# Key and value tiles of a 512-token block: split before eviction, rate operations in short pieces, zeros and a few operations moved into the load phase

## The chip, the cores and the metric

One core of a Trainium2 chip. The metric is the device time of one execution, in microseconds, as the median of three runs.

## The reference

Two stacks of layers over 512 tokens of width 1024, in fp32. What matters here is the start: an attention layer with a compressed, a selected and a windowed branch, and behind it a state-space layer whose rates come from its parameters alone.

```
h = x
y = nsa_mixer(rmsnorm(h, l0_norm), l0_w_in, cmp_k_*, cmp_v_*, l0_w_out)
#   q, kc, vc, ks, vs, kw, vw, gates, z = split(hn @ w_in)
#   k_cmp = silu(blocks(kc) @ w1) @ w2, v_cmp alike: windows of 32 tokens, stride 16
h = h + y
y = s5_mixer(rmsnorm(h, l1_norm), ...)
#   dt = exp(log_dt); ab = exp(lambda * dt), complex: exp, sin, cos of [64, 64] parameters
#   coef = (ab - 1) / lambda; then a scan with powers of ab
h = rmsnorm(h + y, final_norm)
#   then two more layers (attention, gated linear attention) with gated feed-forwards
```

## The kernel before, in words

**Weights.** All weights are a stream of 288 tiles of 128 x 1024, in the order of the stages. SP loads tile t into raw[t mod 4] as soon as POOL has finished with what lay there. Every product is three fp32r matmuls of a high and a low half: DVE's `split_tile` copies raw into whi[t mod 2] (L171), POOL subtracts to get wlo[t mod 2] (L163, waits for w_hi), PE runs 24 matmuls of 512 columns per tile (three per chunk of 128, eight chunks) into one of two accumulators and counts `tile_done`. Since whi and wlo hold two tiles, DVE splits tile u + 2 once PE is through tile u, and PE needs POOL's low half of it one tile later.

**The first stage, nsa_kv,** has eight such tiles (keys and values of three branches; L1154 to L1156). The activations' high halves come from ACT (L1328), the low halves from DVE (L389). The gates are a small fp32 product in front of tile 0 and in its middle (L1140), whose weights `wgate` DVE first multiplies by the norm's gains (L1490). The norm's factor `rstd` needs all squares (ACT L224, DVE L237, PE L244 and L246), so tiles are multiplied by it afterwards: DVE's eviction (L1513) takes acc times rstd, to a bank for u < 4, to nk for the others, and frees the accumulator. For u < 4, ACT copies the high half, kvc_h (`high(u)`, L1347), and DVE subtracts the low half, kvc_l (L1518). After two tiles, ACT issues eight copies between SBUF tiles (`windows(0)`, then `windows(1)`, L1354) that lay out the windows x2 for the compression; they need zeros at the rims (n_zero). nmix is the gates times rstd (L1504).

**The second stage, cmp,** has eight tiles again, two per output, with matmuls of 160 columns (L1184 to L1186); it needs all sixteen copies. Beside it DVE and ACT redo the activations with rstd in them (L1532, L1537, L1360). Then comes nsa_rest, in wide matmuls again (L180 to L182).

**Beside these stages** DVE computes the rates of the state-space layer: some hundred operations on 128 x 32 elements, each of which waits for the one before it (`after_last`; L2157, L2161, L2165). `s5_early(dve, u)` hangs a piece of them behind each tile: u = 0 to 7 are the key and value tiles, 8 to 11 the first four of nsa_rest. Pieces before the change: u = 0 fraction (9 operations), 1 step (7), 2 magnitude (14), 3 angles reduced (13), 4 angles doubled (13 with its polynomial), 5 coefficients (18), 6 powers 0 to 2 (14), 8, 9 and 10 two powers each (12). Tile 4 has four more small ones for the position tables (L1524, L1526). The exponent's power of two is ACT's (L2142).

**What sets the order:** each engine runs its own list as written, and waits only on semaphores. A wait holds everything behind it on its engine; a DMA issue on ACT's queue holds what ACT does later. The loads before the start are issued by SP (weights tile 0, the two halves of x, weights tiles 1 to 3) and ACT (gains, tables, wgate, par, d, then nsa_tables, w2, pe).

Of the kernel before, what the change touches and what calls it, by code (L numbers as in the profile page):

```python
# [47 lines left out]
def build(nc, A, out, names=tuple(s[0] for s in STAGES)):  # L48
# [5 lines left out]
    with ExitStack() as ctx:  # L54
# [1077 lines left out]
        def nsa_loads(act):  # L1132
            for to, what in ((ntab, "nsa_tables"), (w2, "w2"), (pe_in, "pe")):
                act.dma_start(to[:], A[what]).then_inc(n_loaded, 16)

        def pe_nsa(pe):
# [4 lines left out]

            pe.wait_ge(n_wgate, 17)
# [23 lines left out]
            pe.wait_ge(n_loaded, 48)  # L1166
# [156 lines left out]
        def act_first_norm(act):  # L1323

            act.wait_ge(loaded, 32)

            def high(m):
                nc.scalar.activation(xh[:, m, :], h[:, m, :], ACT.Copy,  # L1328
                                     scale=gains[:, N_NSA, m:m + 1]).then_inc(norm_hi, 1)

            act.wait_ge(x_landed[0], 16)
            for m in range(4):
                high(m)
            for m in range(3):
                act_square(act, 0, m)
            act.wait_ge(x_landed[1], 16)
            for m in range(4, KC):
                high(m)
            for m in range(3, KC):
                act_square(act, 0, m)  # L1340
            act_rstd(act, 0)
            act_s5_pow2(act)

        def act_nsa(act):
# [24 lines left out]
            for u in range(3):  # L1369
                high(u)  # L1370
# [3 lines left out]
            act.wait_ge(n_zero, 8)  # L1374
            windows(0)
# [104 lines left out]
        def dve_nsa_begin(dve):  # L1480

            for kv in range(2):
                for part in range(2):
                    nc.vector.memset(x2[kv][part][:, 0:4, S - 1:S + 16].bitcast(F32), 0.0).then_inc(n_zero, 1)
                    nc.vector.memset(x2[kv][part][:, 4, :].bitcast(F32), 0.0).then_inc(n_zero, 1)
            nc.vector.memset(kcb[:], 0.0).then_inc(n_zero, 1)
            nc.vector.memset(vcb[:], 0.0).then_inc(n_zero, 1)
# [12 lines left out]
            for m in range(3, KC - 1):  # L1500
                dve_square_sum(dve, 0, m)
            s5_exponent(dve)
            dve.wait_ge(rstd_ready, 1)
            nc.vector.tensor_tensor(nmix[0:48, :], bank[2][0:48, :], rstd[0:48, :], ALU.mult).then_inc(n_gmm, 1)  # L1504

        def dve_nsa(dve):
            T = T0["nsa_kv"]
            for u in range(8):
                dve.wait_ge(tile_done, T + u + 1)
                if 2 <= u < 4:  # L1510
# [4 lines left out]
                split_tile(dve, (u + 2) % 4, (T + u + 2) // 4)  # L1515
# [4 lines left out]
                if u == 4:  # L1520
                    dve.wait_ge(n_loaded, 48)
# [148 lines left out]
        def pool_nsa(pool):  # L1670
# [8 lines left out]
            def slope(i):  # L1679
                if i == 0:  # L1680
                    pool.wait_ge(n_loaded, 48)
# [454 lines left out]
        def s5_early_loads(act):  # L2136
            for to, what in ((par, "s5_par"), (sd, "s5_d")):
                act.dma_start(to[:], A[what]).then_inc(s_loaded, 16)
# [41 lines left out]
        def s5_exponent(dve):  # L2180

            dve.wait_ge(s_loaded, 32)
# [20 lines left out]

        def s5_magnitude(dve):

            polynomial(dve, ee, xx, [1.0 / FACT[k] for k in range(7, 0, -1)])
# [4 lines left out]
        def s5_angles_reduced(dve):  # L2211
# [52 lines left out]
        def s5_coefficients(dve):  # L2264
# [8 lines left out]
            nc.vector.reciprocal(den, den).then_inc(s_par, 1)  # L2273
            for to, a, b, op in ((cre, nr, abim, ALU.add), (cim, abim, nr, ALU.subtract)):
# [520 lines left out]
        def _(pe):  # L2795
            pe.wait_ge(loaded, 32)
# [203 lines left out]
```

## Time and profile before

| | |
|---|---|
| median of 3 runs | 2107.71 us (2105.72 to 2107.86) |
| profiled execution | 2108.85 us, span 2107.1 us |
| mean granted TensorE clock | 0.972 |
| PE, busy share of the span | 95% |
| DVE, ACT, POOL | 55%, 29%, 38% |
| DMA | 167.64 MB, mean 80 GB/s |

The span is the time from the first to the last instruction of the profiled execution; the execution's own time has 1.75 us more around it. PE's busy share counts matmuls that wait in the pipeline too, so the stretches and the idle times in front of single instructions say more.

### The profile page before, as it was taken

What the parts mean: (1) busy time and instruction counts of PE and PEld (TensorE: products, weight loads), DVE (VectorE), ACT (ScalarE), POOL (GpSimd) and SP (SyncE); (2) the same over time, 40 slices, a digit from 0 to 9 for tenths busy, and PEclk for the clock granted to TensorE, in tenths of its full rate; (3) what the DMA queues carried; (4) which work ended last, traced back from release to release, by engine and by line L of the source; (5) the groups of instructions that cost most, each with busy time, mean ns of one, the idle gap of its engine ahead of it and who ended that gap; (6) DMA issues with size and microseconds to landing.
All of it is one profiled execution on the core that took longest, in us unless ns stands there. A gap on an engine that the chain in (4) does not pass through costs nothing.

```text
span 2107.1 us, 26825 instructions
## 1 busy us (share of the span) xinstructions
PE 1991.7 (95%) x9916; PEld 1562.5 (74%) x9916; DVE 1148.8 (55%) x2072; ACT 607.4 (29%) x1164; POOL 810.9 (38%) x420
## 2 busy tenths in 40 slices
PE   7999999787998996999999999999899999999999
PEld 4877777566777874666668888888578778888887
DVE  6748998576996434555465444522443355445411
ACT  3125566222553113454432111100332222111100
POOL 2441221244774443222224444444233334444444
PEclk9789999999999998999999999999999999999999
DMA  4520010111201222111112222233222222222231
GB/s 163 157 91 31 31 41 31 61 69 54 79 31 51 92 98 77 59 61 60 60 51 92 100 98 91 100 105 105 72 70 70 79 71 92 100 92 97 100 128 72
DMA packets 55300, 167.64 MB, mean 80 GB/s; under 512 B 8080, under 2 KB 16144, under 8 KB 54816
## 3 DMA queue, kind: packets, MB, share of 16 engines
q1 hardware_dynamic: 47904, 155.22, 21.3%
q10 hardware_dynamic: 7296, 11.08, 1.8%
q8 instruction: 65, 1.06, 0.2%
q14 instruction: 35, 0.29, 0.0%
HBM read 157.88 MB, written 2.10 MB: 76 GB/s over the span
## 4 chain that ended last, share of the span: by engine, by line
issue 40%; PE 32%; POOL 15%; DVE 10%; SPq 2%; ACT 0%; POOLq 0%; DMA 0%; DVEq 0%; ACTq 0%
POOL wlo L163 14%; PE bank L180 7%; PE bank L182 7%; PE bank L181 6%; SPq L145 2%; DVE prob L1628 2%; DVE ssb L1615 1%; PE bank L2576 1%; PE bank L2578 1%; PE bank L2577 1%; DVE sb__134 L2391 1%; DVE sb__134 L2386 1%; PE bank L1260 1%; PE bank L1285 1%; DVE sp__133 L2389 1%
## 5 line engine op out<-in xcount | busy, mean ns | idle before, releaser
L163 POOL TENSOR_TENSOR wlo<-raw,whi 128x1024 fp32r<-128x1024 f32 x252 | 606.5, 2407 | 990.4 <-DVE whi L171 990.4
L171 DVE CAST whi<-raw 128x1024 fp32r<-128x1024 f32 x288 | 203.4, 706 | 430.0 <-PE bank L182 235.3
L180 PE MATMUL bank<-xh,whi 128*128 128x512 f32 x704 | 277.0, 393 | 9.3 <-POOL wlo L163 9.3
L181 PE MATMUL bank<-xl,whi 128*128 128x512 f32 x704 | 275.9, 392 | 0.0
L182 PE MATMUL bank<-xh,wlo 128*128 128x512 f32 x704 | 275.6, 391 | 0.0
L595 PE MATMUL bank<-xh,whi 128*128 128x512 f32 x424 | 177.3, 418 | 1.5 <-POOL wlo L163 1.5
L597 PE MATMUL bank<-xh,wlo 128*128 128x512 f32 x424 | 165.9, 391 | 0.0
L596 PE MATMUL bank<-xl,whi 128*128 128x512 f32 x424 | 165.3, 390 | 0.0
L180 PEld LDWEIGHTS bank<-xh,whi 128*128 128x128 f32 x704 | 133.5, 190 | 38.3 <-POOL wlo L163 10.6
L181 PEld LDWEIGHTS bank<-xl,whi 128*128 128x128 f32 x704 | 133.6, 190 | 27.8
L182 PEld LDWEIGHTS bank<-xh,wlo 128*128 128x128 f32 x704 | 133.4, 190 | 28.0
L180 PE MATMUL bank<-ghi,whi 128*128 128x512 f32 x352 | 136.9, 389 | 0.0
L181 PE MATMUL bank<-glo,whi 128*128 128x512 f32 x352 | 136.9, 389 | 0.0
L182 PE MATMUL bank<-ghi,wlo 128*128 128x512 f32 x352 | 136.9, 389 | 0.0
L1676 POOL TENSOR_TENSOR wlo<-raw,whi 128x1024 fp32r<-128x1024 f32 x20 | 47.2, 2359 | 154.8 <-DVE whi L171 154.8
L595 PEld LDWEIGHTS bank<-xh,whi 128*128 128x128 f32 x424 | 79.7, 188 | 27.9 <-issue 13.4
L597 PEld LDWEIGHTS bank<-xh,wlo 128*128 128x128 f32 x424 | 79.6, 188 | 17.8
L596 PEld LDWEIGHTS bank<-xl,whi 128*128 128x128 f32 x424 | 79.9, 188 | 16.3 <-issue 2.2
L1628 DVE TENSOR_SCALAR prob<-prob,gsig,stat 128x128 f32<-128x128 f32 (+3 forms) x128 | 87.2, 723 | 2.3
L477 DVE TENSOR_TENSOR upad<-bank,rstd 128x512 f32<-128x512 f32 x44 | 30.5, 692 | 102.4 <-PE bank L182 87.4
L224 ACT ACTIVATE bank<-h 128x512 f32<-128x512 f32 x42 | 25.2, 602 | 209.7 <-DVE h L401 200.9
L490 DVE TENSOR_TENSOR bank<-bank,rstd 128x512 f32<-128x512 f32 x44 | 30.8, 700 | 99.5 <-PE bank L182 94.2
(384 smaller groups left out, 4030.9 us busy)
## 6 DMA issues: line engine op xcount, KB each, us to landing
raw<-in_weights_dram SPq DMA_DIRECT2D x288, 512.0 KB, 3.2
h<-in_x_dram SPq DMA_DIRECT2D x2, 1024.0 KB, 7.5
sz<-su SPq DMA_DIRECT2D x128, 16.0 KB, 1.8
out_dram<-h ACTq DMA_DIRECT2D x4, 512.0 KB, 2.6
etab<-in_even_tables_dram ACTq DMA_DIRECT2D x1, 1730.0 KB, 6.4
x_kh<-kvc_h ACTq DMA_DIRECT2D x2, 256.0 KB, 3.6
x_kl<-kvc_l ACTq DMA_DIRECT2D x2, 256.0 KB, 7.1
x_vh<-kvc_h ACTq DMA_DIRECT2D x2, 256.0 KB, 7.1
```

The source lines that it names most:

```text
L145: sp.dma_start(sz[32 * r:32 * r + 32, j, q * P:(q + 1) * P], su[32 * q:32 * q + 32, j, r * P:(r + 1) * P]).then_inc(s_ub[j % 4], 16)
L163: nc.gpsimd.tensor_tensor(wlo[:, s % 2, :], raw[:, s, :], whi[:, s % 2, :].bitcast(F32), ALU.subtract).then_inc(w_lo, 1)
L171: nc.vector.tensor_copy(whi[:, t_of_4 % 2, :], raw[:, t_of_4, :]).then_inc(w_hi, 1)
L180: nc.tensor.matmul(to, w_h, pe_h, start=first and k == 0, stop=False)
L181: nc.tensor.matmul(to, w_h, pe_l, start=False, stop=False)
L182: last_mm = nc.tensor.matmul(to, w_l, pe_h, start=False, stop=last and k == chunks - 1)
L490: nc.vector.tensor_tensor(gv, acc[1][:], rstd[:], ALU.mult).then_inc(acc_free[1], 1)
L595: nc.tensor.matmul(to[:], w_h, xh[:, k, :], start=k == 0, stop=False)
L596: nc.tensor.matmul(to[:], w_h, xl[:, k, :], start=False, stop=False)
L597: mm = nc.tensor.matmul(to[:], w_l, xh[:, k, :], start=False, stop=k == KC - 1)
L1628: mul = nc.vector.tensor_scalar(prob[:, br, hd, 0:w], prob[:, br, hd, 0:w], gsig[:, qb, g:g + 1], stat[:, 8 + 2 * br + hd:9 + 2 * br + hd] ...
L1676: nc.gpsimd.tensor_tensor(wlo[:, r % 2, :], raw[:, r % 4, :], whi[:, r % 2, :].bitcast(F32), ALU.subtract).then_inc(w_lo, 1)
```

## The change

1. In `dve_nsa` the split of tile u + 2 stands before the eviction of tile u, and nmix behind the first eviction.
2. The rate operations are cut anew. Exponent and fraction (2 and 9 operations) come before DVE's first wait for the loads, step (7) at the end of `dve_nsa_begin`. Then u = 0 exponential (7), 1 magnitude (7), 2 angles reduced (8), 3 sine and cosine (9), 4 angles doubled (9), 5 coefficients (7), 6 input coefficients (11), 7 nothing, 8 powers 0 to 2 (14), 9, 10 and 11 two powers each (12).
3. The ten memsets for n_zero move from DVE to POOL, ahead of its stream.
4. ACT's loads: par, gains, wgate, tables, ..., d last; ACT's power of two comes before its first wait for the loads.
5. PE runs four fp32 matmuls of 512 columns on a zeroed tile before the gates; its wait for the loads at the top is gone.
6. On ACT, `windows(0)` stands behind `high(1)` instead of behind the gates' sigmoid, so ahead of `high(2)`.

```diff
         def pe_nsa(pe):
...
+            pe.wait_ge(acc_free[0], 1)
+            pe.wait_ge(acc_free[1], 1)
+            for _ in range(4):
+                nc.tensor.matmul(acc[1][:], xf[:, 0, 0:P], xf[:, 0, :], start=True, stop=True)
             pe.wait_ge(n_wgate, 17)
...
         def act_first_norm(act):
 
+            act_s5_pow2(act)
             act.wait_ge(loaded, 32)
...
             act_rstd(act, 0)
-            act_s5_pow2(act)
...
-            for u in range(3):
-                high(u)
+            high(0)
+            high(1)
+            act.wait_ge(n_zero, 8)
+            windows(0)
+            high(2)
             nc.scalar.activation(bank[6], rstd[:], ACT.Copy).then_inc(n_gs, 1)
             act.wait_ge(n_gmm, 2)
             nc.scalar.activation(gsig[:].rearrange("p b g -> p (b g)"), bank[3][:, 0:4 * 48], ACT.Sigmoid).then_inc(n_gs, 1)
-            act.wait_ge(n_zero, 8)
-            windows(0)
             high(3)
             windows(1)
...
-        def dve_nsa_begin(dve):
+        def pool_zeros(pool):
...
+        def dve_nsa_begin(dve):
+
+            s5_exponent(dve)
+            s5_fraction(dve)
             dve.wait_ge(loaded, 32)
             dve.wait_ge(n_wgate, 16)
...
-            s5_exponent(dve)
-            dve.wait_ge(rstd_ready, 1)
-            nc.vector.tensor_tensor(nmix[0:48, :], bank[2][0:48, :], rstd[0:48, :], ALU.mult).then_inc(n_gmm, 1)
+            s5_step(dve)
 
         def dve_nsa(dve):
             T = T0["nsa_kv"]
             for u in range(8):
                 dve.wait_ge(tile_done, T + u + 1)
+                split_tile(dve, (u + 2) % 4, (T + u + 2) // 4)
+                if u == 0:
+                    dve.wait_ge(rstd_ready, 1)
                 if 2 <= u < 4:
                     dve.wait_ge(n_kvh, u - 1)
                     dve.wait_ge(n_kvl, u - 1)
                 nc.vector.tensor_tensor(bank[4 + u % 2] if u < 4 else nk[:, u - 4, :], acc[u % 2][:], rstd[:],
                                         ALU.mult).then_inc(acc_free[u % 2], 1)
-                split_tile(dve, (u + 2) % 4, (T + u + 2) // 4)
+                if u == 0:
+                    nc.vector.tensor_tensor(nmix[0:48, :], bank[2][0:48, :], rstd[0:48, :], ALU.mult).then_inc(n_gmm, 1)
...
         @block.gpsimd
         def _(pool):
             if "s5_in" in names:
+                pool_zeros(pool)
                 pool_stream(pool, 0, T0["nsa_rest"])
...
         @block.scalar
         def _(act):
+            s5_early_loads(act)
             act.dma_start(gains[:], A["gains"]).then_inc(loaded, 16)
+            act.dma_start(wgate[:], A["wgate"]).then_inc(n_wgate, 16)
             act.dma_start(tables[:], A["tables"]).then_inc(loaded, 16)
-            act.dma_start(wgate[:], A["wgate"]).then_inc(n_wgate, 16)
-            s5_early_loads(act)
...
         @block.tensor
         def _(pe):
-            pe.wait_ge(loaded, 32)
...
+            nc.vector.memset(xf[:, 0, :], 0.0)
```

What it moves on DVE, from the end of the first norm (spt, par: rate operations; whi<-raw: the split; bank<-bank,rstd: the eviction). Before:

```order
L2161 TENSOR_SCALAR spt<-spt 128x32
L1504 TENSOR_TENSOR nmix<-bank,rstd 48x512
L1513 TENSOR_TENSOR bank<-bank,rstd 128x512
L171 CAST whi<-raw 128x1024
L1518 TENSOR_TENSOR kvc_l<-bank,kvc_h 128x512
L2165 SCALAR_TENSOR_TENSOR spt<-spt,par 128x32
L2165 SCALAR_TENSOR_TENSOR spt<-spt 128x32
L2161 TENSOR_SCALAR spt<-spt 128x32
L2165 SCALAR_TENSOR_TENSOR spt<-spt 128x32 x6
L1513 TENSOR_TENSOR bank<-bank,rstd 128x512
```

And with the change:

```order
L2168 TENSOR_TENSOR spt<-par,spt 128x32
L2172 TENSOR_SCALAR spt<-spt 128x32
L171 CAST whi<-raw 128x1024
L1524 TENSOR_TENSOR bank<-bank,rstd 128x512
L1527 TENSOR_TENSOR nmix<-bank,rstd 48x512
L1530 TENSOR_TENSOR kvc_l<-bank,kvc_h 128x512
L2172 TENSOR_SCALAR spt<-spt 128x32
L2176 SCALAR_TENSOR_TENSOR spt<-spt 128x32 x6
L171 CAST whi<-raw 128x1024
L1524 TENSOR_TENSOR bank<-bank,rstd 128x512
```

The split is ahead of the eviction in every tile, and nine operations after kvc_l are seven.

On ACT behind the first norm (kvc_h<-bank: `high`; DMA x_kh, x_kl: `windows(0)`; x_vh, x_vl: `windows(1)`). Before:

```order
L256 ACTIVATE rstd<-lnv 128x512
L2142 ACTIVATE spt<-spt 128x32
L1347 ACTIVATE kvc_h<-bank 128x512 x3
L1371 ACTIVATE bank<-rstd 128x512
L1373 ACT_TABLE_LOAD
L1373 ACTIVATE gsig<-bank 128x192
L1354 DMA x_kh<-kvc_h 64x2x512 x2
L1354 DMA x_kh<-kvc_h 64x2x511 x2
L1354 DMA x_kl<-kvc_l 64x2x512 x2
L1354 DMA x_kl<-kvc_l 64x2x511 x2
L1347 ACTIVATE kvc_h<-bank 128x512
```

And with the change:

```order
L256 ACTIVATE rstd<-lnv 128x512
L1351 ACTIVATE kvc_h<-bank 128x512 x2
L1358 DMA x_kh<-kvc_h 64x2x512 x2
L1358 DMA x_kh<-kvc_h 64x2x511 x2
L1358 DMA x_kl<-kvc_l 64x2x512 x2
L1358 DMA x_kl<-kvc_l 64x2x511 x2
L1351 ACTIVATE kvc_h<-bank 128x512
L1378 ACTIVATE bank<-rstd 128x512
L1380 ACT_TABLE_LOAD
L1380 ACTIVATE gsig<-bank 128x192
L1351 ACTIVATE kvc_h<-bank 128x512
```

Eight copies stand between the second and the third kvc_h.

## Rows read from the trace of the kernel before

**Rows 1.** The page's row of the granted clock, 40 equal slices, tenths.
```profile
PEclk9789999999999998999999999999999999999999
```

**Rows 2.** Stretches: length, busy us (count) of PE, PEld, DVE, ACT, POOL, clock, DMA, GB/s.
```profile
35.05:38.05 3.00, 0.00 (x1) 0.00 (x0) 2.93 (x3) 0.57 (x1) 2.34 (x1) 1.00 0.00 0
38.05:41.60 3.55, 3.54 (x9) 2.77 (x10) 3.21 (x11) 0.60 (x1) 0.47 (x1) 0.53 0.46 152
...
67.85:69.03 1.18, 0.17 (x1) 0.00 (x0) 1.18 (x1) 0.00 (x0) 1.13 (x1) 1.00 1.07 239
...
74.60:76.66 2.06, 0.18 (x1) 0.00 (x0) 2.03 (x2) 0.00 (x0) 1.84 (x1) 1.00 0.00 0
76.66:79.20 2.54, 2.51 (x18) 2.54 (x19) 2.16 (x12) 0.00 (x0) 0.00 (x0) 1.00 0.56 200
79.20:82.99 3.79, 1.56 (x9) 1.34 (x8) 3.75 (x7) 1.19 (x2) 2.35 (x1) 0.50 0.02 9
82.99:119.10 36.11, 36.11 (x169) 36.11 (x170) 13.06 (x20) 6.48 (x13) 16.60 (x7) 0.50 0.31 108
119.10:123.50 4.40, 4.40 (x12) 3.43 (x12) 0.69 (x1) 0.54 (x2) 2.36 (x1) 0.50 0.19 74
```

**Rows 3.** Timeline of DVE at tile 0: start, length, instruction, idle before it.
```profile
33.70 0.68 DVE L1504 TENSOR_TENSOR nmix<-bank,rstd 48x512 f32<-48x512 f32 x1 [8.68 <-ACT rstd L256]
...
35.66 0.69 DVE L1518 TENSOR_TENSOR kvc_l<-bank,kvc_h 128x512 fp32r<-128x512 f32 x1
36.26 1.79 DVE L2165 SCALAR_TENSOR_TENSOR spt<-spt,par 128x32 f32<-128x32 f32 x1
...
38.52 1.32 DVE L2165 SCALAR_TENSOR_TENSOR spt<-spt 128x32 f32<-128x32 f32 x6
```

**Rows 4.** The same view at tile 6's eviction, DVE and POOL.
```profile
72.72 0.68 DVE L1513 TENSOR_TENSOR nk<-bank,rstd 128x512 f32<-128x512 f32 x1
...
73.32 0.69 DVE L171 CAST whi<-raw 128x1024 fp32r<-128x1024 f32 x1
...
74.09 2.35 POOL L163 TENSOR_TENSOR wlo<-raw,whi 128x1024 fp32r<-128x1024 f32 x1 [5.11 <-DVE whi L171]
```

**Rows 5.** The same view of the start: two issues on ACT's queue, DVE's first wait.
```profile
1.67 0.45 ACTq L2752 DMA_DIRECT2D wgate<-in_wgate_dram  x1
...
2.16 0.59 ACTq L2138 DMA_DIRECT2D par<-in_s_par_dram  x1
...
11.19 0.56 DVE L1490 TENSOR_TENSOR wgate<-wgate,gains 128x384 f32<-128x384 f32 x1 [7.21 <-DMA wgate<-in_wgate_dram]
```

**Rows 6.** DMA issues up to 20 us: KB each, us from issue to landing.
```profile
wgate<-in_wgate_dram ACTq DMA_DIRECT2D x1, 192.0 KB, 9.4
...
par<-in_s_par_dram ACTq DMA_DIRECT2D x1, 48.0 KB, 10.4
```

**Rows 7.** Timeline of PE: the gates' passes, before tile 0 and in it.
```profile
11.85 6.54 PE L1140 MATMUL bank<-h,wgate 128*48 128x512 f32 x8 [11.85 <-DVE wgate L1490]
21.27 3.63 PE L1140 MATMUL bank<-h,wgate 128*48 128x512 f32 x8
```

**Rows 8.** Timeline of ACT and its queue: the first copy of windows(0), then high(3).
```profile
46.22 0.72 ACTq L1354 DMA_DIRECT2D x_kh<-kvc_h  x1
...
53.83 0.60 ACT L1347 ACTIVATE kvc_h<-bank 128x512 fp32r<-128x512 f32 x1 [4.95 <-issue]
```

**Rows 9.** Instructions on kvc_l: count, ns of one min/median/max, first and last start.
```profile
L1354 ACTq DMA_DIRECT2D x_kl<-kvc_l x4: 628/913/1794, 49.4 to 53.2; - x4
L1354 ACTq DMA_DIRECT2D x_vl<-kvc_l x4: 636/710/942, 58.1 to 60.6; - x4
...
DMA to landing us min/median/max: 6.7/8.3/12.0
```

**Rows 10.** Timeline of DVE: its split behind the fourth tile of nsa_rest.
```profile
151.53 0.69 DVE L171 CAST whi<-raw 128x1024 fp32r<-128x1024 f32 x1 [6.12 <-PE bank L597]
```

More of the change, by code:

```diff
@@ L1132, in nsa_loads @@
         def nsa_loads(act):
-            for to, what in ((ntab, "nsa_tables"), (w2, "w2"), (pe_in, "pe")):
+            for to, what in ((ntab, "nsa_tables"), (w2, "w2"), (pe_in, "pe"), (sd, "s5_d")):
                 act.dma_start(to[:], A[what]).then_inc(n_loaded, 16)
@@ L1164, in pe_nsa @@
                     mm.then_inc(n_gmm, 1)
-            pe.wait_ge(n_loaded, 48)
+            pe.wait_ge(n_loaded, 64)
             pe.wait_ge(n_x2, 16 * 16)
@@ L1478, in act_macro @@
                 act_exps(act, M + 1, 1)
-        def dve_nsa_begin(dve):
+        def pool_zeros(pool):
             for kv in range(2):
                 for part in range(2):
[L1484 to L1487, printed above, removed]
+                    nc.gpsimd.memset(x2[kv][part][:, 0:4, S - 1:S + 16].bitcast(F32), 0.0).then_inc(n_zero, 1)
+                    nc.gpsimd.memset(x2[kv][part][:, 4, :].bitcast(F32), 0.0).then_inc(n_zero, 1)
+            nc.gpsimd.memset(kcb[:], 0.0).then_inc(n_zero, 1)
+            nc.gpsimd.memset(vcb[:], 0.0).then_inc(n_zero, 1)
+        def dve_nsa_begin(dve):
+            s5_exponent(dve)
+            s5_fraction(dve)
             dve.wait_ge(loaded, 32)
@@ L1520, in dve_nsa @@
                 if u == 4:
-                    dve.wait_ge(n_loaded, 48)
+                    dve.wait_ge(n_loaded, 64)
                     for kv in range(2):
@@ L1680, in slope @@
                 if i == 0:
-                    pool.wait_ge(n_loaded, 48)
+                    pool.wait_ge(n_loaded, 64)
                 if i >= 2:
@@ L2136, in s5_early_loads @@
         def s5_early_loads(act):
-            for to, what in ((par, "s5_par"), (sd, "s5_d")):
-                act.dma_start(to[:], A[what]).then_inc(s_loaded, 16)
+            act.dma_start(par[:], A["s5_par"]).then_inc(s_loaded, 16)
         def act_s5_pow2(act):
@@ L2180, in s5_exponent @@
         def s5_exponent(dve):
-            dve.wait_ge(s_loaded, 32)
+            dve.wait_ge(s_loaded, 16)
             ts(dve, kk, lg_dt, 1.4426950408889634, MAGIC, ALU.mult, ALU.add)
@@ L2202, in s5_step, with s5_exponential @@
             ts(dve, xx, xx, -80.0, 1.0 / 64, ALU.max, ALU.mult)
+        def s5_exponential(dve):
+            polynomial(dve, ee, xx, [1.0 / FACT[k] for k in range(7, 0, -1)])
         def s5_magnitude(dve):
-            polynomial(dve, ee, xx, [1.0 / FACT[k] for k in range(7, 0, -1)])
             for _ in range(6):
@@ L2273, in s5_coefficients, with s5_input_coefficients @@
             nc.vector.reciprocal(den, den).then_inc(s_par, 1)
+        def s5_input_coefficients(dve):
             for to, a, b, op in ((cre, nr, abim, ALU.add), (cim, abim, nr, ALU.subtract)):
@@ L2331, in s5_early @@
             if u == 0:
-                s5_fraction(dve)
+                s5_exponential(dve)
             if u == 1:
-                s5_step(dve)
+                s5_magnitude(dve)
             if u == 2:
-                s5_magnitude(dve)
+                s5_angles_reduced(dve)
             if u == 3:
-                s5_angles_reduced(dve)
+                s5_sine_cosine(dve)
             if u == 4:
@@ L2343, in s5_early @@
             if u == 6:
+                s5_input_coefficients(dve)
+            if u == 8:
                 s5_powers(dve, 0, 2)
-            if u == 8:
+            if u == 9:
                 s5_powers(dve, 3, 4)
-            if u == 9:
+            if u == 10:
                 s5_powers(dve, 5, 6)
-            if u == 10:
+            if u == 11:
                 s5_powers(dve, 7, 8)
```

3 lines of the change are left out of this document (2 added, 1 removed).

## The prediction

> **What bounds the kernel now.** The page's clock row comes first: PEclk is 9 nearly everywhere and lower in slices 2 and 3, where the change lies [rows 1]; from there on I read only the first 151 us. The view by stretches [rows 2] shows where PE loses time: 3.00 us idle before key and value tile 2 (35.05 to 38.05), then 3.55 us with the clock at half; 1.18 us idle before tile 7; 2.06 us before the first compression tile; 2.23 us (3.79 less 1.56) before the second, at 82.99; then 36.11 us of 160-column matmuls at half clock, seven tiles of 5.15, and 4.40 us of wide ones before the clock is back.
>
> The timeline says why. DVE evicts a tile, splits the next weights but one, subtracts kvc_l, then does rate operations; POOL can make the low half, and PE can go on, only behind the split. Tile 2's split stood behind nmix, which came at 33.70 after 8.68 us for rstd, and behind tile 0's eviction [rows 3], though tile 0 was complete near 27.6 (the gates end at 24.9 [rows 7], and twelve matmuls of 0.227 follow). Later the rate operations make DVE late: tile 6 left PE at 67.85 [rows 2] and was evicted at 72.72 [rows 4]. A round of DVE there is 0.60 from eviction to split, 0.77 to POOL's start, 2.35 of POOL [rows 4], and meanwhile the rate operations stand still: L2165 took 1.79 us, against 0.22 each when POOL rests (six in 1.32), while kvc_l, which reads a PSUM bank and one SBUF tile, took its usual 0.69 beside POOL [rows 3, 4]. A tile is 24 matmuls, 5.45 us; a round with 13 operations is 6.5, and PE pays the difference.
>
> **The change, part by part.**
>
> *Loads.* On ACT's queue wgate, third, landed at 11.1 and par, fourth, at 12.55 (issue plus time to landing) [rows 5, 6]. Now the order is par, gains, wgate, tables. DVE and ACT wait for gains and tables, so both start when the fourth has landed; the four are the same 400 KB, so I take the fourth's time. DVE began at 11.19 [rows 5]: **+1.35 us**. Bounds: 0, if tables took wgate's time; +4.2, if it came two more turns of 1.45 late. ACT waits for the same, but its first high is there at 13.3, when DVE has scaled wgate (0.5) and split (0.6) and asks for it, and DVE's lows stay the slower chain.
>
> *PE kept busy.* Four fp32 matmuls of 512 columns are eight passes of 0.82 at the half clock (the gates' eight take 6.54, at full clock 3.63) [rows 7]: from about 1.6 to 8.3. The gates start at 13.2 (11.85 + 1.35). The idle 5 us between is longer than the 3.00 after which the clock was at half [rows 2], so I cost the warm-up at **0**; the other bound is -2.9 (6.54 - 3.63). It delays nothing, since it ends before the gates' data is there.
>
> *Zeros to POOL, pow2 and eleven rate operations early.* Ten memsets go to POOL, whose first split comes near 13.7, and pow2 and 11 operations (11 x 0.22 = 2.4 us) lie in the time in which DVE waited for wgate, 7.21 us [rows 5]. Cost 0; the cover is par, now first to land: if it came after 10, what is left over would add to the start. s5_step (7 operations, 1.5 us) goes into the 8.68 us of waiting for rstd [rows 3].
>
> *Split before eviction.* Tile 1 ends at 35.05 or a little before, now 1.35 later, 36.25; tile 2's low half is ready by 32.5, and its bank at 35.7 (rstd at 33.7 + 1.35, eviction 0.6). PE goes straight on, at full clock. What goes is the idle stretch, 3.15 with its rim, and half of the 3.55 at half clock: **-3.15 and -1.75 us**. An eviction now starts just behind the split, at the moment POOL starts. No row has an eviction beside POOL; kvc_l has the same kind of operands and is not held. If it were held, it would end 0.8 + 2.4 + 0.6 = 3.8 after the tile, still within 5.45. The Trainium skill, "SBUF — State Buffer", section "SBUF: two separate sides", says that only DVE operations with two SBUF inputs or in a two-port mode are shut out by GpSimd; by it the eviction is free, and the sum is the same by either.
>
> *Shorter pieces.* A round is now 0.75 + 2.39 + 0.22n (less 0.1 at its end). For u = 3 to 6, n = 9, 13 (four of them on the position tables), 7, 11: 5.0 + 5.9 + 4.6 + 5.5 = 21.0 against 21.8 of PE. The idle 6.6 us from tile 3 on (0.25 before tile 6, 1.18 and 0.1, 2.06 and 0.1, 2.23, and 0.65 for compression tile 0's half clock) would go but for what follows.
>
> *Windows(0) ahead of high(2).* This is the new wait. ACT issues eight copies, 46.22 to 53.8, 0.95 each, and nothing behind them runs: high(3) came out at 53.83, after 4.95 of issue [rows 8]. They now stand before high(2), and DVE's kvc_l(2) waits for high(2), with eight rate operations and the split for tile 5 behind it. Working: rstd is there at 35.05 and DVE is through u = 0 at 38.7 (eviction and nmix 1.2, high and kvc_l 1.3, seven operations 1.5 less 0.1, 0.25 of hand-overs); split(3), POOL ends 41.9 (PE waits 0.2); kvc_l(1) ends 41.3; copies to 48.9; high(2) 49.5; kvc_l(2) 50.2; operations 51.9; split(5) and POOL 55.0. PE, after tile 2, four transposes (0.45), tiles 3 and 4, is at 53.2: **1.8 us idle** (0.2 if a copy costs 0.71, 8 if each cost 1.79, the shortest median and the longest [rows 9]).
>
> *To the end of the stage.* Split(9) follows split(5) by 21.0: 72.9, POOL done 76.05. PE is through tile 7 at 55.05 + 3 x 5.45 = 71.4 (tiles 5 to 7) and through compression tile 0 (24 x 0.144, from 18 in 2.54 [rows 2]) at 74.9: **1.15 us idle**. The second compression tile starts at 76.05, before at 82.99. The rest of the stage runs at half clock, 5.15 us a tile as before [rows 2], **-0.5** because its first matmuls still find the full clock (0 to -1.7). The powers, now at r = 0 to 3 with 14, 12, 12, 12 operations: DVE sat idle for 6.12 before its split at 151.53 [rows 10], so the twelve (2.7) at r = 3 and two more at r = 0 are hidden.
>
> **Sum:** +1.35 - 3.15 - 1.75 + 0.2 - 6.6 + 1.8 + 1.15 - 0.5 = **-7.5 us**. The profiled execution took 2108.85, 1.1 above the median of 2107.71; -7.5 on the median is 2100.2. A measurement of this kernel tells about 0.2%, 4.2 us, from no change.
>
> **Rivals.**
> *A. The compression tiles stay at the full clock.* The clock fell at 79.20, 2.5 us into them, after 2.06 idle, and narrow matmuls did not bring it back in 36 us; 1.18 idle between wide tiles did not bring it down [rows 2]. If the 1.15 us vanishes, or does no harm, seven tiles take 3.45 to 3.5 instead of 5.15 (POOL's round of 3.2 just keeps up): -11.6, and the 4.40 us at half after them give 2.2. Time 2100.2 - 13 = 2087. For it: a longer stall at tile 5 lets DVE catch up, so the gap can close. Against: DVE's sum leaves it open in my working. The skill's "TensorE: Matmul & The Clock Gate", section "HAM oscillation — how this bites in real kernels", names PE-idle gaps as what throttles; by its rule a gap as short as the 1.18 that did no harm keeps the clock, and the time would be this rival's. Chance 0.22.
> *B. The warm-up carries over to the gates,* or tables lands with wgate's time: 2.9 or 1.35 more, 2097. Chance 0.08.
> *C. Given back:* tables lands two turns later than forecast (+2.9) and one more stretch runs 3.55 us at half (+1.8): 2104.9. Chance 0.06.
> *D. Slower: ACT's copies.* At 1.79 each, the longest row, windows(0) ends at 55.6, windows(1) runs from 61 to 75.4, and its last copy, 8.3 to landing [rows 9], is there near 82. PE needs it for the first compression tile, which began at 76.66; the second follows at 86 instead of 82.99: 2107.7 + 3.3 = 2111. It decides once a copy costs over 1.2 in both groups (before, 0.95 and 0.71). Chance 0.04.
>
> **Numbers.** Forecast 0.60, with its own range 2097 to 2103.3 (below: loads at 0, a copy at 0.71, so 1.35 and 1.6 less; above: loads one turn later, 1.45, and a copy at 1.1, 1.2 more). To hold 8 in 10 the range has to reach to A: 2086.5 to 2103.3. Faster by over 4.2 us: A, B, and nearly all of the forecast, 0.88; same 0.08; slower 0.04.
>
> **What would show it.** DVE's first operation on wgate near 12.5; eight warm-up passes ending before 8.4 and gates again at 0.82 a pass; no idle time before tile 2; ACT's high(2) behind eight copies and PE waiting 1 to 2 us for wlo at tile 5; 1.2 us before the second compression tile, and clock 0.50 from there to the wide tiles. I am wrong if the compression stage shows clock 1.00 (A), if gates start before 12, or if kvc_l(2) does not wait.

## The result, and the profile after

| | before | changed |
|---|---|---|
| median of 4 runs each, same chip | 2106.72 us (2105.35 to 2107.86) | 2085.03 us (2082.57 to 2086.61) |
| ratio, 95% interval | | 0.9896 [0.9879, 0.9913] |
| profiled execution (span) | 2108.85 (2107.1) | 2086.61 (2084.8) |
| mean granted TensorE clock | 0.972 | 0.981 |

The change saves 21.7 us, 1.04% (0.87 to 1.21). The forecast was 2100.2 with a range down to 2086.5; the result lies 1.5 us below the range. It is nearly what rival A gave (2087).

The busy slices of PE and the clock row of the page after, against [rows 1]. Each digit is a fortieth of the span, 52 us:

```profile
## 2 busy tenths in 40 slices
PE   8999999778999997999999999999999999999999
...
PEclk9999999998999998999999999999999999999999
```

The clock is 9 in slices 2 and 3, where it was lower before. The 8 in slice 10 (469 to 521 us) costs the change nothing that shows: both kernels have such dips in that part (0.79 and 0.83 before, from 492 to 510 us; 0.79, 0.84 and 0.74 changed, from 468 to 492), and the lead in the table below is no smaller at the end. The view by stretches shows slices 1 and 2, from 33.75 us on, closely (columns: length, busy time of PE, PE's weight load, DVE, ACT and POOL with their instructions, granted clock, DMA share, GB/s):

```profile
33.75:51.63 17.88, 17.88 (x81) 14.51 (x80) 11.13 (x33) 3.91 (x6) 5.12 (x3) 1.00 0.62 152
51.65:53.72 2.07, 0.37 (x2) 0.00 (x0) 1.39 (x3) 0.60 (x1) 2.02 (x1) 1.00 1.03 223
53.72:70.22 16.50, 16.50 (x73) 13.62 (x73) 15.46 (x42) 0.00 (x0) 7.19 (x3) 1.00 0.96 231
70.22:74.10 3.88, 3.61 (x26) 3.35 (x24) 3.77 (x9) 1.17 (x2) 2.39 (x1) 1.00 0.31 118
74.10:78.09 3.99, 3.66 (x25) 3.41 (x25) 3.10 (x6) 1.51 (x5) 2.38 (x1) 1.00 0.42 131
78.09:98.96 20.87, 20.87 (x144) 20.63 (x145) 10.58 (x16) 5.02 (x10) 14.29 (x6) 1.00 0.46 152
98.96:104.53 5.57, 5.57 (x26) 4.61 (x25) 0.69 (x1) 0.54 (x2) 2.39 (x1) 1.00 0.45 142
```

Tiles 2 to 4 run without a gap; tile 5 waits (second row); the compression stage (70.22 to 98.96) is at 1.00 throughout, its last six tiles in 20.87 us, 3.48 each, where seven took 5.15 each before [rows 2]. In PE's timeline of the changed kernel, these are all the matmuls before 110 us that begin after idle time (start, duration, engine and line, operation, shapes, then idle time and what ended it):

```profile
1.58 6.33 PE L1145 MATMUL bank<-xf 128*128 128x512 f32 x8 [1.58 <-DVE seedt L2846]
12.49 5.94 PE L1140 MATMUL bank<-h,wgate 128*48 128x512 f32 x8 [4.58 <-DVE wgate L1500]
53.72 0.50 PE L1158 MATMUL bank<-xh,whi 128*128 128x512 f32 x1 [1.70 <-POOL wlo L163]
74.10 0.39 PE L1188 MATMUL bank<-x_kh,whi 128*128 128x160 f32 x1 [0.27 <-POOL wlo L163]
78.09 0.39 PE L1188 MATMUL bank<-x_kh,whi 128*128 128x160 f32 x1 [0.33 <-POOL wlo L163]
```

From the starts of the tiles in PE's two timelines comes the account of the gain:

| PE starts | before | changed | lead | came in since the line above |
|---|---|---|---|---|
| second gates | 21.27 | 21.31 | -0.04 | |
| gates' transposes, behind tile 2 | 45.31 | 40.46 | 4.85 | 4.89: stall and half clock at tile 2 |
| tile 5 | 56.70 | 53.72 | 2.98 | -1.87: the new wait |
| first compression tile | 76.69 | 70.22 | 6.47 | 3.49: idle time |
| second compression tile | 82.99 | 74.10 | 8.89 | 2.42: idle time 2.23 to 0.27, and the clock |
| nsa_rest | 118.92 | 98.96 | 19.96 | 11.07: the clock |
| first scores | 153.67 | 131.58 | 22.09 | 2.13: the clock of the wide tiles behind it |
| end of the span | 2107.1 | 2084.8 | 22.3 | 0.2 |

So 13.2 of 22.3 us are the clock behind the second compression tile. The next section shows what it hangs on.

DVE's timeline of the changed kernel: its multiply of wgate, the split of tile 2 (27.93), the first eviction (L1524), kvc_l(2), which reads what high(2) made (48.28, L1530), the splits (L171) of tile 5 and the four behind it, and one more eviction:

```profile
11.87 0.56 DVE L1500 TENSOR_TENSOR wgate<-wgate,gains 128x384 f32<-128x384 f32 x1 [4.91 <-DMA tables<-in_tables_dram]
...
27.93 0.69 DVE L171 CAST whi<-raw 128x1024 fp32r<-128x1024 f32 x1 [1.09 <-PE bank L1160]
33.75 0.70 DVE L1524 TENSOR_TENSOR bank<-bank,rstd 128x512 f32<-128x512 f32 x1 [5.13 <-ACT rstd L256]
...
48.28 0.69 DVE L1530 TENSOR_TENSOR kvc_l<-bank,kvc_h 128x512 fp32r<-128x512 f32 x1 [5.35 <-ACT kvc_h L1351]
...
50.54 0.69 DVE L171 CAST whi<-raw 128x1024 fp32r<-128x1024 f32 x1
...
55.43 0.69 DVE L171 CAST whi<-raw 128x1024 fp32r<-128x1024 f32 x1
...
60.92 0.69 DVE L171 CAST whi<-raw 128x1024 fp32r<-128x1024 f32 x1
...
65.56 0.63 DVE L171 CAST whi<-raw 128x1024 fp32r<-128x1024 f32 x1
...
70.88 0.69 DVE L171 CAST whi<-raw 128x1024 fp32r<-128x1024 f32 x1
71.49 0.68 DVE L1524 TENSOR_TENSOR nk<-bank,rstd 128x512 f32<-128x512 f32 x1
```

Tile 2's split comes at 27.93, where before it came behind 33.7 [rows 3]. The four rounds between the last five splits are 4.89, 5.49, 4.64 and 5.32 us. The eviction at 71.49 is not held by POOL, which made the low half from 71.65 to 74.04 (no row before showed that pair).

ACT's timeline of the changed kernel (ACTq: issues of its DMA queue):

```profile
39.91 4.03 ACTq L1358 DMA_DIRECT2D x_kh<-kvc_h  x4
43.97 3.64 ACTq L1358 DMA_DIRECT2D x_kl<-kvc_l  x4
47.65 0.60 ACT L1351 ACTIVATE kvc_h<-bank 128x512 fp32r<-128x512 f32 x1 [8.56 <-issue]
...
57.13 3.48 ACTq L1358 DMA_DIRECT2D x_vl<-kvc_l  x4
```

high(2) stood behind eight copies as forecast, 0.96 us each, and came at 47.65.

### The profile page after: what moved, and what is told of

The parts are those of the page before. It is cut to its first block, busy times and chain, and to the rows that moved or that the text cites. A ratio compares the mean times of both kernels' runs of the same rounds, so it can differ in the third digit from the quotient of the medians.

```text
span 2084.8 us, 26851 instructions
## 1 busy us (share of the span) xinstructions
PE 1981.5 (95%) x9924; PEld 1549.0 (74%) x9924; DVE 1143.3 (55%) x2063; ACT 608.3 (29%) x1164; POOL 813.7 (39%) x430
## 3 DMA queue, kind: packets, MB, share of 16 engines
q8 instruction: 65, 1.06, 0.2%
## 4 chain that ended last, share of the span: by engine, by line
issue 40%; PE 33%; POOL 15%; DVE 11%; ACT 1%; POOLq 0%; DVEq 0%; ACTq 0%
POOL wlo L163 14%; PE bank L180 7%; PE bank L181 7%; PE bank L182 7%; DVE prob L1640 2%; DVE ssb L1627 1%; PE bank L2598 1%; PE bank L2600 1%; PE bank L2599 1%; DVE wtmp L2168 1%; PE bank L1264 1%; DVE sb__134 L2413 1%; DVE sb__134 L2408 1%; PE bank L1289 1%; DVE sp__133 L2411 1%
## 5 line engine op out<-in xcount | busy, mean ns | idle before, releaser
L171 DVE CAST whi<-raw 128x1024 fp32r<-128x1024 f32 x288 | 203.4, 706 | 407.8 <-PE bank L182 237.4
```

The costliest lines, as they stand in the source:

```text
L171: nc.vector.tensor_copy(whi[:, t_of_4 % 2, :], raw[:, t_of_4, :]).then_inc(w_hi, 1)
```

## The experiments

**Theory T:** the compression stage (tiles of 160-column matmuls, called narrow below; those of 512 columns are wide) keeps the full clock when PE has little idle time ahead of its first tiles, and falls to half, for the whole stage, when it has more; the change saves 13 us by closing those gaps. **Rival R:** the gaps don't matter; another part of the change decides, the missing half-clock stretch at tile 2 for one. Beside this, each part's own worth was open. "Before" in each line is the kernel before on the same chip.

### Fillers in the kernel before (e5)

```diff
+                    if o == 0:
+                        for _ in range((20, 24)[q]):
+                            nc.tensor.matmul(bank[2][:, 0:5 * NW], x2[0][0][:, 0, 0:P],
+                                             x2[0][0][:, :, 0:16 * NW - 15:16], start=True, stop=True)
                     pe.wait_ge(w_lo, t0 + 2 * o + q + 1)
```

> The kernel before, with nothing of the change, but PE multiplies 20 and 24 extra 160-column matmuls (results unused, into bank 2) while it waits for the low halves of the first and the second compression tile, in the gaps of 2.06 and 2.23 us. Theory T (what takes the clock down in the compression tiles is PE's idle time just ahead of them): the clock stays at 1.00 from 76.7 on, seven tiles take 3.5 us each instead of 5.15, and the time is 13 to 14 us shorter, 2093 to 2094. Rival R (the change's other parts, such as the absence of the earlier half-clock stretch, or the narrow matmuls themselves, decide): the clock falls near 79 as before and the time stays at 2107, give or take 1.

Measured: 2093.0 us (2091.4 to 2096.0), before 2105.98; ratio 0.9933 [0.9907, 0.9959]. Stretches of this run, the second to fourth with the bounds of [rows 2]:

```profile
74.40:76.69 2.29, 2.29 (x18) 2.29 (x17) 2.12 (x6) 0.00 (x0) 1.22 (x1) 1.00 0.03 7
76.69:79.20 2.51, 2.51 (x20) 2.51 (x18) 2.27 (x10) 0.00 (x0) 0.00 (x0) 1.00 0.59 209
79.20:82.99 3.79, 3.79 (x29) 3.79 (x28) 3.75 (x6) 1.65 (x3) 2.40 (x1) 1.00 0.00 0
82.99:107.00 24.01, 24.01 (x168) 23.83 (x168) 12.24 (x19) 6.03 (x13) 16.05 (x7) 1.00 0.47 154
```

PE was busy all the time and the clock stayed at 1.00; nothing else of the change is in this kernel, whose tile 2 still waits its 3.0 us. 13.0 us saved by work that no one uses: R falls as an account of these 13 us, and the clock's price is measured by itself.

### Idle time put back into the changed kernel (e6, e7, e11)

```diff
                 s5_input_coefficients(dve)
+                for _ in range(6):
+                    tt(dve, t1, lam_re, lam_im, ALU.mult)
```

> The changed kernel with 6 extra rate operations of DVE (results unused) at u = 6, 0.22 us each, so that the split for the second compression tile comes about 1.3 us later and PE's idle time there is about 1.6 us instead of 0.33. Theory T with a harmless gap up to at least 1.18: the clock still holds, 2085 + 1.3 = 2086.3. If 1.6 us is enough to bring it down: 2085 + 1.3 + 13 = 2099. Rival R (idle time has nothing to do with it): 2086.3 as well.

> The changed kernel with 12 extra rate operations at u = 6: idle time of PE ahead of the second compression tile about 2.9 us. Theory T: the clock falls to 0.50 some 2 us into the compression tiles and stays there to the wide ones; 2085 + 2.6 + 13 = 2101. Rival R: the clock holds and only the wait is added, 2088.

> The changed kernel with 3 extra rate operations at u = 6: some 0.9 us of idle time of PE ahead of the second compression tile, between the 0.27 of the changed kernel (clock held in every run) and the 1.43 of the evict-first run (fell in most). Theory: the clock holds in every run, and the time is 0.7 us longer, 2085.7. If the margin is smaller than I think, some or all runs are near 2098.

(These texts place the changed kernel's 0.27 and 0.33 us ahead of the first and second compression tile; the rows above put them ahead of the second and third.) PE's row at the second compression tile, with 6, with 12 and with 3 extra operations:

```profile
75.63 0.50 PE L1188 MATMUL bank<-x_kh,whi 128*128 128x160 f32 x1 [1.59 <-POOL wlo L163]
```

```profile
76.09 0.50 PE L1188 MATMUL bank<-x_kh,whi 128*128 128x160 f32 x1 [2.96 <-POOL wlo L163]
```

```profile
74.13 0.39 PE L1188 MATMUL bank<-x_kh,whi 128*128 128x160 f32 x1 [0.99 <-POOL wlo L163]
```

| idle time | median | runs | ratio to before |
|---|---|---|---|
| 1.59 us | 2099.1 | ten, 2096.2 to 2103.6 | 0.9967 [0.9953, 0.9981] |
| 2.96 us | 2100.87 | ten, 2096.7 to 2104.0 | 0.9967 [0.9955, 0.9978] |
| 0.99 us | 2097.56 | four 2096.7 to 2098.0, one 2088.9 | 0.9948 [0.9929, 0.9967] |

With 0.99 us of idle time (0.7 more than in the changed kernel) the time grows by 12. The idle times are those of one profiled run of each kernel; the other runs are sorted by time and mean clock. The stretches with 3 extra operations:

```profile
73.10:74.13 1.03, 0.04 (x2) 0.01 (x1) 1.02 (x2) 0.97 (x2) 0.97 (x1) 1.00 0.00 0
74.13:76.00 1.87, 1.87 (x11) 1.87 (x11) 1.83 (x4) 0.63 (x2) 0.31 (x1) 0.67 0.40 112
76.00:109.50 33.50, 33.50 (x159) 33.50 (x158) 11.75 (x18) 5.89 (x12) 16.30 (x7) 0.50 0.32 107
```

The clock fell within 1.9 us of the gap, and then 33.5 us of uninterrupted matmuls (PE busy 33.50 of 33.50) ran at half clock. Theory T holds, but not the margin I gave it: the expectation for 0.99 us (clock held in every run) was a miss. The rule I had taken from 1.18 us between wide tiles [rows 2] does not carry over to narrow ones; in every profile here with a gap of 1.2 to 1.7 us before the wide tile 5 the clock stayed at 1.00.

### The changed kernel again (e12)

> The changed kernel, unaltered, on the same chip as the three below, so that they can be compared with it. 2085, give or take 2, with the clock at 1.00 in the compression stage in every run.

Measured: 2085.48 us, before 2105.23, ratio 0.9905 [0.9887, 0.9924]; five runs 2080.9 to 2086.3 and one of 2092.4 with a mean clock of 0.980 where the others have 0.983 or 0.984. So the changed kernel may stand near the edge. That is not shown: the slow one was not profiled, and the profile of the changed kernel above has a mean clock of 0.981 with the whole stage at 1.00. The expected "clock at 1.00 in every run" is confirmed for the two profiled runs, and the times make it likely for seven more of the ten.

### Copies back behind the sigmoid (e1)

```diff
             high(1)
-            act.wait_ge(n_zero, 8)
-            windows(0)
             high(2)
...
+            act.wait_ge(n_zero, 8)
+            windows(0)
             high(3)
```

> The changed kernel with windows(0) back behind the sigmoid, so that high(2) is not behind eight copies on ACT. Theory: PE's 1.70 us of idle time at tile 5 go; DVE gets 1.7 us less slack, so some of it comes back as idle time ahead of the first and second compression tiles (0.27 and 0.33 now, up to 1.2 together more); if the clock holds, 2084 to 2085; if that gap brings it down, 2097 to 2098. Rival (DVE is late there for its own reasons and the stall at tile 5 covers nothing): 2083.3 with unchanged gaps.

Measured: 2099.67 us (2096.3 to 2104.7), ratio 0.9969 [0.9955, 0.9982]. The number is near one of the expected ones, the cause is another. Tile 5 no longer waits, but PE's row at the first compression tile, and the rows on x_vl (the last four copies: lengths of an issue in ns, first and last start, and the time to landing), read:

```profile
71.19 0.36 PE L1188 MATMUL bank<-x_kh,whi 128*128 128x160 f32 x1 [2.85 <-issue]
```

```profile
L1358 ACTq DMA_DIRECT2D x_vl<-kvc_l x4: 637/641/772, 54.9 to 57.0; - x4
...
DMA to landing us min/median/max: 9.6/11.3/14.1
```

"issue" is a wait that the profile gives no releaser for; here it is the one for the sixteen copies, whose last is issued at 57.0 and lands 14.1 later, at 71.1. In the changed kernel the same rows read:

```profile
L1358 ACTq DMA_DIRECT2D x_vl<-kvc_l x4: 639/864/1027, 57.1 to 59.6; - x4
...
DMA to landing us min/median/max: 6.3/8.0/9.4
```

59.6 + 9.4 = 69.0 at the latest, 1.2 us before PE wants them. Copies issued later, but over a longer time, landed earlier. Why they did is not shown: the 16 DMA engines were full of weights and copies in both kernels (share 1.06 from 53.0 to 68.3 us here, 0.96 from 53.7 to 70.2 in the changed kernel), so what the weight stream moved just then may count as much as the spacing of the issues. In this combination, moving windows(0) ahead costs 1.7 us at tile 5 and brings the landing ahead of PE, and with it the clock: a net gain of 14 us.

### The pieces and the split's place, each undone (e2, e3)

e2 has the pieces of before (14, 13, 17, 18, 14 operations at u = 2 to 6, powers at u = 8 to 10) behind the split that comes first. e3 keeps the short pieces:

```diff
                 if u == 0:
                     dve.wait_ge(rstd_ready, 1)
+                    nc.vector.tensor_tensor(nmix[0:48, :], bank[2][0:48, :], rstd[0:48, :], ALU.mult).then_inc(n_gmm, 1)
                 dve.wait_ge(tile_done, T + u + 1)
-                split_tile(dve, (u + 2) % 4, (T + u + 2) // 4)
...
                                         ALU.mult).then_inc(acc_free[u % 2], 1)
+                split_tile(dve, (u + 2) % 4, (T + u + 2) // 4)
```

> The changed kernel with the rate operations in the pieces of before (14 operations at u = 2, 13 at u = 3, 13 and the four on the position tables at u = 4, 18 at u = 5, 14 at u = 6, 12 at u = 8 to 10); the split stays ahead of the eviction. Theory: a round is 3.14 + 0.22 n us, so those of u = 3 to 6 take 6.0, 6.9, 7.1 and 6.2, 26.2 in all against 21.8 of PE; 4 to 5 us of idle time return between tile 6 and the second compression tile, and with over 1.5 us of them ahead of the compression tiles the clock falls there: 2085 + 4.5 + 12.5 = 2102. If the clock holds in spite of it: 2089.5.

> The changed kernel with the eviction (and for tile 0 nmix) ahead of the split again; pieces, loads and copies stay. Theory: the 3.0 us of idle time before tile 2 and its half-clock stretch return, 4.9 us; a round is about 0.6 longer where the pieces are long (5.7, 6.6, 5.3 and 6.1 for u = 3 to 6, 23.7 against 21.8 of PE), so that some 1.5 to 2 us of idle time stand ahead of the compression tiles and the clock falls: 2085 + 4.9 + 1.9 + 12.5 = 2104. If the clock holds: 2092. If split before eviction brought nothing: 2085.

Measured: long pieces 2102.57 us (2099.5 to 2106.7), ratio 0.9983 [0.9973, 0.9994]; eviction first 2099.34 us, ratio 0.9959 [0.9939, 0.9979]. PE's idle rows, for the long pieces from tile 6 on (ahead of tile 5 it waited 1.42 us), for eviction first from tile 2 on:

```profile
65.20 0.50 PE L1158 MATMUL bank<-xh,whi 128*128 128x512 f32 x1 [0.60 <-POOL wlo L163]
72.49 0.36 PE L1188 MATMUL bank<-x_kh,whi 128*128 128x160 f32 x1 [1.52 <-POOL wlo L163]
78.42 0.50 PE L1188 MATMUL bank<-x_kh,whi 128*128 128x160 f32 x1 [1.43 <-POOL wlo L163]
```

```profile
39.07 0.64 PE L1158 MATMUL bank<-xh,whi 128*128 128x512 f32 x1 [3.01 <-POOL wlo L163]
79.10 0.39 PE L1188 MATMUL bank<-x_kh,whi 128*128 128x160 f32 x1 [1.43 <-POOL wlo L163]
```

The long pieces bring back 3.6 us of idle time, and the half clock (0.50 from 74.5 us on). Eviction first brings back tile 2's 3.01 us, and 1.43 us at the second compression tile. Its ten runs range from 2088.9 (clock 0.980) to 2106.2 (0.970), which suggests that a gap of that size brings the clock down in most executions and not in all; only one of the ten was profiled, and in it the clock fell. Without either part most of the gain is lost; with both the clock keeps.

### The warm-up taken out (e4)

```diff
-            for _ in range(4):
-                nc.tensor.matmul(acc[1][:], xf[:, 0, 0:P], xf[:, 0, :], start=True, stop=True)
             pe.wait_ge(n_wgate, 17)
```

> The changed kernel without the four warm-up matmuls. Theory: the gates' eight passes take 6.5 us again instead of 5.9, and nothing else moves: 2085.6. If the warm-up is worth nothing at all: 2085.0. If the clock later depends on it: over 2095.

Measured: 2088.34 us (2085.8 to 2089.6), ratio 0.9916 [0.9896, 0.9935]. That is 3 us over the changed kernel and over the expected 2085.6, but the ratios' intervals overlap, so the time alone can't say. The traces can, at the place itself: from the first gates to the second it took 9.42 us in the profile before, 9.13 in e5 and 9.41 here; with the four warm-up matmuls it took 8.17 to 9.48 in nine profiles, 8.75 in the mean. Their worth is 0.6 us on average, and between executions it varies by more. What the rest of the 3 us is, if it is more than noise, stays open.

### Copies in halves, input coefficients moved (e8)

```diff
-            windows(0)
+            windows(0, 0)
             high(2)
+            windows(0, 1)
...
             high(3)
-            windows(1)
+            windows(1, 0)
+            windows(1, 1)
```

Here windows(kv, 0) issues the four copies of kvc_h and waits for n_kvh alone; `s5_input_coefficients` goes from u = 6 to behind the last split of the compression tiles.

> The changed kernel with the copies issued in halves, those of kvc_h ahead of high(2) and those of kvc_l behind it (for v the high half right behind high(3)), and the 11 operations of the input coefficients moved from u = 6 to the time in which DVE waits behind the last split of the compression tiles (4.89 us idle). Theory: high(2) comes some 3.6 us earlier, the 1.70 us of idle time at tile 5 shrink to 0.2 or less, the round of u = 6 takes 3.1 us, so that the 0.27 and 0.33 us ahead of the compression tiles go too and the clock holds: 2085 - 1.7 - 0.5 = 2082.8. If the copies land too late for the first compression tile (as they did with windows(0) behind the sigmoid, 2.85 us): the clock falls and the time is 2097.

Measured: 2083.56 us (2081.4 to 2085.0), ratio 0.9895 [0.9876, 0.9914], not to be told from the changed kernel's by time. nsa_rest starts at 96.63 instead of 98.96. Tile 5 doesn't wait. What waits instead is in PE's timeline and in the rows on x_vl:

```profile
68.87 0.36 PE L1188 MATMUL bank<-x_kh,whi 128*128 128x160 f32 x1 [0.62 <-issue]
```

```profile
L1358 ACTq DMA_DIRECT2D x_vl<-kvc_l x4: 634/637/637, 52.4 to 54.4; - x4
...
DMA to landing us min/median/max: 11.2/12.3/14.4
```

54.4 + 14.4 = 68.8: the last copy again, issued 5.2 us earlier than in the changed kernel and landed 0.2 earlier. The landing now sets when the stage begins. With 0.62 us of idle time at the first compression tile the clock stayed at 1.00 in the profile, and the other three runs, at 0.982 and 0.983 in the mean, look the same.

### An earlier start (e9, e10), and its gap filled (e13)

On top of e8, DVE and ACT no longer wait for tables; seven warm-up matmuls in e9, four in e10:

```diff
-            act.dma_start(gains[:], A["gains"]).then_inc(loaded, 16)
+            act.dma_start(gains[:], A["gains"]).then_inc(n_wgate, 16)
...
-            act.wait_ge(loaded, 32)
+            act.wait_ge(n_wgate, 32)
...
-            dve.wait_ge(loaded, 32)
-            dve.wait_ge(n_wgate, 16)
+            dve.wait_ge(n_wgate, 32)
...
+                        pe.wait_ge(loaded, 16)
                         pe_squares(pe, 0)
```

> The run with the copies in halves and the input coefficients behind the compression tiles (2083.6), with two edits at the start: DVE and ACT wait for the gains and wgate alone, no longer for tables (PE waits for tables ahead of its sums of squares), and seven warm-up matmuls in place of four, to end just ahead of the gates. Theory: wgate lands at 10.2 and tables at 11.9, so DVE's multiply starts 1.7 us earlier; the clock, which rose inside the gates, is at full when they start, and their eight passes take 3.6 us instead of 5.9: 2083.6 - 1.7 - 2.3 = 2079.6. If rstd's chain on ACT and DVE is what sets the time of the stage: 2083.6 - 1.7 at best, 2082.

> The same with four warm-up matmuls as in the changed kernel, which end near 8, more than 2 us ahead of the gates. Theory: only the 1.7 us of the earlier start are left, and the gates take 5.9 us: 2083.6 - 1.7 = 2081.9. If the shorter idle time ahead of the gates (3 us instead of 4.6) lets the clock stay: as with seven, 2079.6.

Measured: e9 2084.16 us, ratio 0.9902 [0.987, 0.9935], three runs of 2078.7 to 2079.4 and three of 2089.0, 2094.0 and 2096.4; e10 2090.19 us, ratio 0.9915 [0.9887, 0.9943], three of 2079.7 to 2084.8 and three of 2095.5 to 2097.6. In e9's profile the gates ran at full clock (first gates at 11.15, second at 17.66, 6.51 us, against 8.8 to 9.5 in the changed kernel), and the compression stage did not:

```profile
11.15 3.63 PE L1140 MATMUL bank<-h,wgate 128*48 128x512 f32 x8 [1.07 <-DVE wgate L1502]
...
66.06 0.36 PE L1189 MATMUL bank<-x_kh,whi 128*128 128x160 f32 x1 [1.37 <-issue]
```

PE is now early enough to wait 1.37 us for the last copy (51.1 + 14.9 = 66.0). The profile of e10 (2095.5, where 2081.9 was expected) has the same wait, shorter, and the clock at 0.50 from 71 us on:

```profile
66.98 0.36 PE L1189 MATMUL bank<-x_kh,whi 128*128 128x160 f32 x1 [0.78 <-issue]
```

Is that gap what costs the clock? e13 fills the one of e9 and changes nothing else:

```diff
             pe.wait_ge(n_loaded, 64)
+            for _ in range(3):
+                nc.tensor.matmul(bank[2][:, 0:256], xf[:, 0, 0:P], xf[:, 0, 0:256], start=True, stop=True)
             pe.wait_ge(n_x2, 16 * 16)
```

> The run with the earlier start and seven warm-up matmuls, and in it three fp32 matmuls of 256 columns (results unused, six passes of 0.23 us, 1.4 us in all) ahead of PE's wait for the position copies. In that run the first compression tile waited 1.37 us for the last copy and the clock fell; three of six runs took 2079, the others up to 2096. Theory: the idle time ahead of the first compression tile is what takes the clock down there; with the fillers in its place the clock holds in every run, and all are near 2079 to 2080. Rival: the runs near 2094 have another cause (the start, or the copies themselves); then runs over 2090 remain.

Measured: 2078.75 us, four runs from 2077.9 to 2079.3, before 2106.37; ratio 0.9867 [0.985, 0.9883]. Its stretches:

```profile
64.00:66.20 2.20, 2.20 (x13) 1.93 (x12) 1.47 (x3) 0.00 (x0) 0.69 (x1) 1.00 0.74 277
66.20:94.00 27.80, 27.80 (x193) 27.42 (x192) 15.71 (x24) 7.94 (x17) 18.37 (x8) 1.00 0.40 133
```

No idle time, clock 1.00, and no run above 2080. This is what the theory says, with idle time from the copies in place of idle time from DVE. It is weaker evidence than e5: three of e9's six runs were at 2079 without the filler, so four of four could be chance. This is the best version found, 27.6 us below the kernel before in its comparison and with every run under all ten of the changed kernel (2080.9 to 2092.4), though on another chip; its ratio's interval lies below that of e12, the changed kernel again, too.

## Why the prediction was wrong, point by point

- **What failed: "The second compression tile" after "1.15 us idle", and "the rest of the stage runs at half clock".** The idle time was 0.27 us, so the rest ran at full clock. Of the 14.7 us between forecast and profile (-7.5 against -22.2, 2108.85 to 2086.61), 12.7 are this: behind the second compression tile 13.2 us came in where 0.5 was forecast. The conclusion from the gap came out (0.99 us brought the clock down in four runs of five), though no row of the kernel before had shown it for so short a gap ahead of narrow matmuls, so that it was in part luck. The gap was mis-sized. It was a difference of two sums near 20 us, and its two terms missed by tenths. DVE's four rounds were to take 5.0, 5.9, 4.6 and 5.5, 21.0 in all, and took 4.89, 5.49, 4.64 and 5.32, 20.34; the round with the four small table operations was 0.4 too dear, and some 0.26 of that is two of them that began before the one ahead had ended. PE's three tiles and the first compression tile were 19.8 by my working and took 20.11. Together that closes 0.9 us of the 1.15. 13 us hung on 0.9, and I gave the side on which they fell 0.22.
- **Rival A** had the right stage, price (13) and nearly the right time (2087). It rested on two reasons. "A longer stall at tile 5 lets DVE catch up, so the gap can close" is what happened, though the stall was as forecast and the rounds were shorter. Its price of 13 left out the gap itself: from its own terms (11.6 and 2.2 less the 0.5 that the forecast had already taken, and 0.9 of idle time) the time would be 2086.0, and with the 1.3 us that the start did not cost 2084.7, where 2085.03 was measured. So the range's lower end, set by A's 2087, lay too high even for A. "A gap as short as the 1.18 that did no harm keeps the clock" is refuted: 0.99 us ahead of a narrow tile did harm, 1.70 ahead of a wide one didn't. The Trainium skill, "TensorE: Matmul & The Clock Gate", section "HAM oscillation — how this bites in real kernels", names PE's idle gaps as the cause; the filler runs agree with that. By its rule, as the prediction used it, 0.99 us should have done no harm; the measurement differs and decides, and the pair 0.99 and 1.70 shows that the length of the gap alone doesn't tell.
- **Loads, +1.35:** DVE's multiply came at 11.87, 0.68 after the 11.19 of before [rows 5], since tables landed then, half a turn earlier than wgate's 1.45 us step foretold. Direction right, size half.
- **Warm-up, 0:** it ended at 7.9, the clock was down again at the gates (0.60 in the mean from 12.49 to 18.40 us), and 0.6 us came back on average. Right in kind. Both together: +0.04 at the second gates instead of +1.35, which is the second part of the miss, 1.3 us.
- **Zeros and early operations, 0:** right. par was there at 4.54 and the eleven operations were through at 7.0, before the gains.
- **Split before eviction, -3.15 and -1.75:** 4.90 forecast, 4.89 measured by the table's second line; evictions beside POOL took their usual 0.68 or 0.69. The Trainium skill, "SBUF — State Buffer", section "SBUF: two separate sides", had said so of operations with a single SBUF input, and the trace agrees.
- **+0.2 before tile 3:** not there.
- **windows(0) ahead, +1.8 at tile 5:** 1.70 us of idle time and 1.87 in the table. Mechanism and size right. What I missed is its other side: without it the last copy lands at 71.1, 2.85 us too late (e1). I priced the wait that it adds and not when the transfers behind it land.
- **Idle time from tile 3 on, -6.6, +1.15:** 5.9 us came in between tile 5 and the second compression tile, 5.3 forecast.
- **Powers behind nsa_rest hidden:** right; the lead stays at 22.1 from 131 us to the end.
- **D (copies at 1.79 each):** the issue took 0.96 and 0.92 us each; the copies were close to late nonetheless, by their 9 to 14 us to landing and not by their issue.
- **The range's upper end:** the terms named for it (1.45 and 1.2) give 2102.9 and not 2103.3; nothing hangs on it.

What I should have written: the chance of the forecast and of rival A closer together, since the sign of a 1.15 us difference between sums of 20 us with terms good to 0.1 or 0.4 each was not known.

## What to carry to other kernels

Where a stage of small matmuls follows a gap, price the gap by what the clock does behind it, not by its length alone: here 0.7 us more of idle time cost 12. When a forecast hangs on such an edge, work out the edge's two sides as two outcomes with like chances, and try a filler: a few unused matmuls ahead of a wait are the cheapest test of whether the clock is the cause, and here they were the cure too (13.0 us in e5). When an issue of transfers is moved, look up when the last of them lands, as well as who waits for the issuing engine.

## What the runs showed that was not expected

- Idle time of PE ahead of a 160-column tile, each read from one profile, the other runs by time and mean clock. Ahead of the first such tile: 0.62 us left the clock up in four of four runs, 0.78 (e10) and 1.37 (e9) in three of six each. Ahead of the second: 0.33 and less in at least nine of ten, 0.99 in one of five, 1.43 in some of ten, 1.59 and 2.96 in none. So there is no single length at which it falls. Ahead of a 512-column tile 1.23 to 1.70 us left it up in all seven profiles with such a gap ahead of tile 5; 3.00 (the kernel before) did not.
- Once at half, the clock stayed there for 33.5 us of matmuls without any idle time, and came back only in the wide ones.
- Sixteen copies between SBUF tiles beside the weight stream: the more closely they were issued, the longer the last took to land, whether for that reason or for another. At 0.64 us apiece it took 14.1 to 14.9 us, at 0.71 (the kernel before) 12.0, at 0.86 (the changed kernel) 9.4; against the changed kernel's 69.0 us, copies issued 5.2 us earlier landed at 68.8 and others issued 2.6 us earlier at 71.1.
